# Moving the low parts of split operands to another start address modulo 512 bytes in SBUF

## What is computed

```python
def reference(x, ...):
    x = first_block(x, ...)    # layer 0: LRU + window attention, dense SwiGLU of width 2816
                               # layer 1: gated delta net, mixture of 8 experts of width 3584, top 2
    return second_block(x, ...)  # twice: SwiGLU of width 2816, conv/gating mixer, SwiGLU of width 2816

def swiglu(h, w_gate, w_up, w_down):
    return (jax.nn.silu(h @ w_gate) * (h @ w_up)) @ w_down
```

## Time and profile before

| | |
|---|---|
| median of the runs | 2406.1 us |
| span of the profiled execution, first to last instruction | 2403.7 us (2.4 us under the median of the runs) |
| PE busy | 2382.4 us, 99% of the span, 12542 matmuls |
| PEld busy | 2017.0 us, 84% |
| DVE busy | 1872.4 us, 78% |
| ACT busy | 1438.0 us, 60% |
| HBM | 597.91 MB read, 252 GB/s over the span |
| PE in the chain that ended last | 94% |

### The profile page before, as it was taken

The page is one execution under the profiler, slowest core; times in us unless marked ns, Lnnn a source line. Parts: engine busy times, 40 slices in busy tenths (PEclk is TensorE's granted clock), DMA queues, the critical chain, the costliest instruction groups (busy, mean ns, idle before and its releaser), DMA issues.

```text
span 2403.7 us, 34175 instructions
## 1 busy us (share of the span) xinstructions
PE 2382.4 (99%) x12542; PEld 2017.0 (84%) x12542; DVE 1872.4 (78%) x1961; ACT 1438.0 (60%) x1474; POOL 14.2 (1%) x34
## 2 busy tenths in 40 slices
PE   8999999999999999999999999999999999999998
PEld 7788899888888888888888888888788888897887
DVE  7767786678888888888888898677966676688666
ACT  6645455567777777777777776555254454544444
POOL 1000000000000000000000010000000000000000
PEclk9999999999999999999999999999999999999999
DMA  8375143459999999999999996853355566533653
GB/s 301 116 251 177 68 147 130 146 207 376 380 377 348 374 379 378 348 377 377 377 348 373 381 395 246 278 177 123 132 193 175 194 227 230 176 126 123 200 191 125
DMA packets 315952, 603.73 MB, mean 251 GB/s; under 512 B 9120, under 2 KB 135200, under 8 KB 315552
## 3 DMA queue, kind: packets, MB, share of 16 engines
q1 hardware_dynamic: 314160, 592.70, 69.1%
q10 hardware_dynamic: 1136, 7.87, 0.8%
q0 software_dynamic: 576, 2.10, 0.2%
HBM read 597.91 MB, written 8.91 MB: 252 GB/s over the span
## 4 chain that ended last, share of the span: by engine, by line
PE 94%; DVE 2%; ACT 1%; DMA 1%; DVEq 1%; issue 0%; SPq 0%; ACTq 0%
PE bank L205 20%; PE bank L206 20%; PE bank L207 19%; PE bank L1218 17%; PE bank L1222 9%; PE bank L3513 1%; PE bank L2955 1%; PE bank L3440 1%; PE bank L2230 1%; PE bank L2240 1%; DMA mslot<-in_e_w_in 1%; PE bank L2930 1%; PE bank L1714 1%; PE bank L1058 0%; PE bank L2149 0%; PE bank L2249 0%
## 5 line engine op out<-in xcount | busy, mean ns | idle before, releaser
L3205 DVE TENSOR_TENSOR weights_lo<-mslot,weights_hi 128x2048 fp32r<-128x2048 f32 x336 | 767.5, 2291 | 117.5 <-ACT weights_hi L3098 116.5
L3098 ACT ACTIVATE weights_hi<-mslot 128x2048 fp32r<-128x2048 f32 x336 | 644.0, 1919 | 217.4 <-PE bank L207 214.2
L1370 DVE TENSOR_TENSOR weights_lo<-scratch,weights_hi 128x2048 fp32r<-128x2048 f32 x165 | 377.2, 2289 | 166.3 <-ACT weights_hi L1363 166.2
L1218 PE MATMUL bank<-x_parts,weights_hi 128*128 128x512 f32 x1760 | 441.2, 392 | 1.8 <-DVE x_parts L921 1.8
L1218 PEld LDWEIGHTS bank<-x_parts,weights_hi 128*128 128x128 f32 x1760 | 319.4, 189 | 63.8 <-DVE x_parts L921 2.4
L205 PE MATMUL bank<-weights_hi,x_pair 128*128 128x512 f32 x896 | 356.9, 398 | 0.2 <-issue 0.2
L206 PE MATMUL bank<-weights_lo,x_pair 128*128 128x512 f32 x896 | 351.4, 392 | 0.0
L207 PE MATMUL bank<-weights_hi,x_pair 128*128 128x512 f32 x896 | 349.9, 391 | 0.0
L1363 ACT ACTIVATE weights_hi<-scratch 128x2048 fp32r<-128x2048 f32 x165 | 315.3, 1914 | 49.3 <-PE bank L207 49.0
L205 PE MATMUL bank<-weights_hi,hidden_hi 128*128 128x512 f32 x808 | 315.9, 391 | 0.0
L206 PE MATMUL bank<-weights_lo,hidden_hi 128*128 128x512 f32 x808 | 315.2, 390 | 0.0
(11 more groups left out here) (561 smaller groups left out, 2735.0 us busy)
## 6 DMA issues: line engine op xcount, KB each, us to landing
mslot<-in_o_moe_w_gate SPq DMA_DIRECT2D x112, 1024.0 KB, 6.8
mslot<-in_o_moe_w_up SPq DMA_DIRECT2D x112, 1024.0 KB, 6.8
mslot<-in_o_moe_w_down SPq DMA_DIRECT2D x112, 1024.0 KB, 6.9
scratch<-in_ffn_w_gate SPq DMA_DIRECT2D x44, 1024.0 KB, 5.2
scratch<-in_ffn_w_up SPq DMA_DIRECT2D x44, 1024.0 KB, 5.1
scratch<-in_ffn_w_down SPq DMA_DIRECT2D x44, 1024.0 KB, 5.0
mslot<-in_o_w_in SPq DMA_DIRECT2D x7, 2048.0 KB, 10.8
scratch<-in_e_ffn_w_gate SPq DMA_DIRECT2D x11, 1024.0 KB, 5.2
```

The costliest lines, as they stand in the source:

```text
L1218: pe.matmul(m.ps[bank + j][:, :], hi[:, k, cols(j)], both, start=(k == 0), stop=False)
L1370: dve.tensor_tensor(m.wlo[to][:, :], m.fslot[i], m.whi[to][:, :], ALU.subtract).then_inc(m.sig["f_lo"], 1)
L3098: act.activation(m.whi[(place + half) % PLACES][:, :], r.slot[slot + half], ACT.Copy).then_inc(s["r_hi"], 1)
L3205: dve.tensor_tensor(m.wlo[i][:, :], r.slot[slot + half], m.whi[i][:, :], ALU.subtract).then_inc(s["r_lo"], 1)
```

## The change

No instruction is added, removed or moved, and no semaphore wait changes: on every engine the same operations stand in the same order with the same shapes. Only addresses in SBUF change. These are the starts in bytes within each partition, modulo 512, as they follow from the widths in `place` (the rows and slices used in the products step by 512 bytes or multiples of it, so that each operand of a matmul has the number of its buffer):

| operand | before | after |
|---|---|---|
| weights_hi, x_parts, hidden_hi, fp32r scratch of the mixers | 64 | 64 |
| weights_lo | 64 | 128 |
| hidden_lo | 64 | 128 |
| x_pair, high half | 256 | 64 |
| x_pair, low half | 256 | 128 |
| mixer_lows (low parts of the mixer's last part) | 256 | 128 |
| mix_parts, mslot | 128 | 128 |
| fslot (raw FFN weights) | 256 | 64 |
| xn_lo | 64 | 64 |

A pad of 16 elements ("phase0") ahead of `weights_lo` and one of 112 behind it ("phase1") do this; `hidden_lo` goes into the room of the first mixer's gate weights `w_a` in `small`, 40 elements into it; `x_pair` gets 16 elements between its halves. The delta net's output product takes its buffers by an offset into `scratch` that keeps them at 64.

```diff
--- before.py
+++ after.py
@@ -48,6 +48,9 @@
 NE, FE = 8, 3584
 FC = 512
 NC = FE // FC
+
+PHASE = 16
+HL_AT = 40
 
 DA, DB, DC = 384, 256, 384
 AT = DA // P
@@ -138,6 +141,8 @@
     m.mslot = [sb(f"mslot{i}", KT * HALF) for i in range(3)]
     m.res = cut(sb("res", NT * D), 0, NT, D)
     consts = sb("consts", CONST_W)
+    with nc.sbuf_tensor("small_parts", [P, SMALL_W], F32R) as small_parts:
+        m.hl = cut(small_parts, SMALL_COLS["w_a"][0] + HL_AT, HALF)
     small = sb("small", SMALL_W)
     small2 = sb("small2", LAYERS2 * SMALL2_W)
     m.consts, m.small, m.small2 = consts, small, small2
@@ -173,24 +178,28 @@
         m.scr = lambda at, *dims: cut(scratch, at, *dims)
     with nc.sbuf_tensor("scratch_parts", [P, R], F32R) as scratch_parts:
         m.scr_parts = lambda at, *dims: cut(scratch_parts, at, *dims)
-    f0 = R - 3 * PIECE
+    f0 = 17408
     m.odd_rows, m.odd_xT = m.scr(21504, NT, D), m.scr(2048, KT, SEQ)
 
     m.splits = {u: i for i, u in enumerate((1, 4, 6, 7, 9))}
     rows = m.xn.rearrange("p t d -> p (t d)")
     m.diag, m.scales = rows[:, 0:SEQ], rows[:, SEQ:2 * SEQ]
-    m.c_raw = [m.scr(f0 + i * KT * DC, KT, DC) for i in range(2)]
+    m.c_raw = [m.scr(f0 + 16 + i * KT * DC, KT, DC) for i in range(2)]
     m.fslot = [m.scr(f0 + i * PIECE, PIECE) for i in range(3)]
 
     m.whi = [sb(f"weights_hi{i}", PIECE, F32R) for i in range(3)]
+    sb("phase0", PHASE)
     m.wlo = [sb(f"weights_lo{i}", PIECE, F32R) for i in range(3)]
+    sb("phase1", P - PHASE)
     m.x2 = cut(sb("x_parts", KT * 2 * SEQ, F32R), 0, KT, 2, SEQ)
     m.xh, m.xl = m.x2[:, :, 0, :], m.x2[:, :, 1, :]
-    m.hh, m.hl = sb("hidden_hi", HALF, F32R), sb("hidden_lo", HALF, F32R)
-    with nc.sbuf_tensor("mixer_lows", [P, f0 + 3 * PIECE - 6 * PIECE - KT * 2 * SEQ - 2 * HALF], F32R) as lows:
-        m.c_low = [cut(lows, f0 - 6 * PIECE - KT * 2 * SEQ - 2 * HALF + i * KT * DC, KT, DC) for i in range(2)]
-    sb("scratch_rest", f0 + PIECE - 6 * PIECE - KT * 2 * SEQ - 2 * HALF)
-    m.xg = cut(sb("x_pair", 2 * PIECE, F32R), 0, 2, KT, 2 * P)
+    m.hh = sb("hidden_hi", HALF, F32R)
+    free = f0 - 6 * PIECE - KT * 2 * SEQ - HALF - P
+    with nc.sbuf_tensor("mixer_lows", [P, free + 16 + 3 * PIECE], F32R) as lows:
+        m.c_low = [cut(lows, free + 16 + i * KT * DC, KT, DC) for i in range(2)]
+    sb("scratch_rest", free + PIECE)
+    xg = sb("x_pair", 2 * PIECE + PHASE, F32R)
+    m.xg = [cut(xg, i * (PIECE + PHASE), KT, 2 * P) for i in range(2)]
     return m
 
 
@@ -496,11 +505,10 @@
     ks = slice(half * KT // 2, (half + 1) * KT // 2)
     wide = lambda t: t.rearrange("p (k n) -> p k n", n=HALF)
     if b == 9:
-        hi = m.xg.rearrange("p i k t -> p (i k t)")[:, PIECE - 48:2 * PIECE - 48] if half == 0 else \
-            m.x2.rearrange("p k i t -> p (k i t)")[:, 0:PIECE]
+        hi = m.scr_parts((21504, 12288)[half], PIECE)
         low = m.b_low
     else:
-        hi = (m.whi[0], m.wlo[1])[half][:, :]
+        hi = (m.whi[0][:, :], m.scr_parts(8192, PIECE))[half]
         low = wide(m.mix[:, 2 * KT * HALF:3 * KT * HALF])
     return mblock(m, B_ODD + b)[:, ks, :], wide(hi), low[:, ks, :]
 
@@ -509,7 +517,7 @@
 
 
     turned = lambda x: x[:, :].rearrange("p (k t) -> p k t", t=SEQ)[:, :, t * P:(t + 1) * P]
-    return odd_mem(m).yT[:, :, t * P:(t + 1) * P], turned(m.wlo[2]), turned(m.wlo[0])
+    return odd_mem(m).yT[:, :, t * P:(t + 1) * P], turned(m.scr_parts(10240, PIECE)), turned(m.scr_parts(6144, PIECE))
 
 
 def odd_out_hi(act, m, b, half):
@@ -2790,7 +2798,7 @@
     flat = lambda t: t.rearrange("p k t -> p (k t)")
     x2 = m.x2.rearrange("p k i t -> p (k i t)")
     r.yh, r.yl = (x2[:, (2 + i) * KT * P:(3 + i) * KT * P] for i in range(2))
-    r.xg = [m.xg[:, i] for i in range(2)]
+    r.xg = m.xg
     xT = flat(m.xT)
     r.silu, r.h = xT[:, 0:FC], xT[:, FC:2 * FC]
     r.oh = m.oh.rearrange("p (t s) -> p t s", t=NT)
@@ -3410,7 +3418,7 @@
     c = Place()
     c.apad = m.scr(4096, AT, PAD_A + SEQ)
     c.sg = c.acc = m.scr(5120, AT, SEQ)
-    c.mixT = m.scr(10240, KT, SEQ)
+    c.mixT = m.scr(10240 + PHASE, KT, SEQ)
     c.g, c.v = m.scr(0, NT, 2 * DB), m.scr(1024, NT, DB)
     c.ccs, c.zacc = m.scr(1536, AT, SEQ), m.scr(13312, AT, SEQ)
     c.zpad = m.scr(14080, AT, PAD_C + SEQ)
```

## The result

The changed kernel takes **2417.6 us** (median of 5 runs, 2417.45 to 2419.08), against 2406.1 us before it (5 runs on the same chip, 2405.7 to 2407.0): a ratio of 1.0047, with a 95% interval from 1.0036 to 1.0057. It is 11.5 us slower, where 12 us less were forecast, and it lies outside the range (2386 to 2401 us).

A forecast was written before the change was run, and what follows sets the result against it. The prediction took PE's matmul pace, set by load-to-stream start offsets, as the bound. It summed 8.0 + 5.4 + 0.9 - 1.2 - 1.1 = 12.0 us, from 2406.1 to 2394 us, with a range for 8 in 10 of 2386 to 2401.

The forecast's parts named there:

- The rival by which they don't: Whole kernel: the address is not the cause of the slower pace, so nothing moves, 2406 us; chance 0.08.
- Step 3: Both downs: hidden_lo and weights_lo go to 128 together, load-to-stream offsets stay 0, 0, 0; zero gain.
- Step 2: Experts' gate and up: all three load-to-stream offsets go from 192 to 0; 896 triples gain 5.4 us.
- Step 1: FFN gate and up: load-to-stream offset goes from 0 to 64, a run of eight from 0.95 to 0.907; gain 8.0 us.
- Step 4: Mixer's last part: 64 triples go to offsets 64, 64, 64, from 0.354 to 0.340 us each; gain 0.9 us.
- Step 5: Last downs with hidden parts in x_parts: 80 triples get offsets 0, 448, 0, from 0.680 to 0.695; loss 1.2 us.
- Step 6: FFN: the 512-column matmul before each narrow run covers a load at offset 64; loss 1.1 us, bounded 0 to 3.3.
- The settling: FFN wide runs after narrow ones: 0.027 us extra expected to stay, not counted; 5.9 us more if it went.
- The third rival: Triples of 512 columns: the moving stream's jump between parts costs 0.015 us on all 896 + 808, giving 2422.8 us; chance 0.08.

The follow-up runs named there:

- wl_back: The changed kernel with weights_lo back at 64, while hidden_lo and x_pair's low half stay at 128; 2418.7 us, ratio to before 1.0052.
- all_at_64: The changed kernel with weights_lo, hidden_lo and both halves of x_pair at 64; 2401.8 us, ratio to before 0.9981.
- map1: A separate small program streaming only fp32r matmuls, with starting bytes as the one variable; 24 matmuls of 512 columns took 5.60 us at offset 64, 5.46 at 256.
- x_back: The changed kernel with hidden_lo and both halves of x_pair at 64, while weights_lo stays at 128; 2422.0 us (one run).
- narrow_alone: The all_at_64 kernel with only the FFN's gate and up low weight parts moved 64 bytes off x_parts; 2398.8 us, ratio to before 0.9969.
- ffn_phases: The all_at_64 kernel with FFN gate and up weights moved: high parts 192 bytes off x_parts, low parts 64; 2393.9 us, ratio to before 0.9949.
- low_256_off: The changed kernel with weights_lo, hidden_lo and x_pair's low half 256 bytes off the high parts instead of 64; 2401.4 us, ratio to before 0.9981.

## Why the prediction was wrong

The bound was read rightly: PE's pace is the time, no wait moved, and the start addresses do set the pace. The rival by which they don't is out: wl_back and all_at_64 differ in the starts of hidden_lo and of x_pair's low half alone, and by 17 us. The sentence of the Trainium skill (TensorE: Matmul & The Clock Gate, Step-by-step: what each phase is for) that a load doesn't steal read bandwidth doesn't carry as far as "addresses are free": the same matmul takes 0.2267 or 0.2333 us in map1, with nothing but the start of the stationary operand changed (L19 and L20).

- **Step 3, "Offsets stay 0, 0, 0. Zero.", is the step that failed.** It took the load's offset against the stream as the whole of the rule. down kept all its offsets and still went from 0.680 to 0.693, +8.2 us. What matters as well is that the triple's starts agree among themselves; a difference of 64 bytes broke that on both operands at once, and either alone costs as much (map1, wl_back, x_back).
- **Step 2** failed by the same rule. The half of it that moved x_pair to the weights' start was right: alone it gives 4.8 us in the sum of the triples (5.4 forecast). The half that spread the low parts cost 9.8 (627.1 against 617.3), so +5.0 came out.
- **Step 1** had the right sign and the wrong size: 0.942 for a run of eight instead of 0.907, 2.1 us over the 210 counted runs instead of 8.0 over 220. Its clean price came from a mixer stretch in which every matmul has the same offset. The FFN's narrow runs stand behind a wide run at offset 0, and behind such a run offset 64 gives 0.118 a matmul; behind one at 192 it gives 0.113 (narrow_alone and ffn_phases).
- **Step 4** gave nothing, 0.353 before and after. There too an offset of 64 in each of three places didn't bring 0.340. The same part has 16 triples with the high parts in `mix_parts`, which the prediction left out: their low parts moved too, and they went from 0.340 to 0.353, 0.2 us lost.
- **Step 5** came out as forecast: a median of 0.696 a triple for 0.695, and 1.0 us lost for 1.2. Its reason, the load at offset 448, isn't shown by that, since the stream jumps in these triples too.
- **Step 6** was too careful: the wide runs in front, the place of its entry, kept their sum (386.2 us against 386.4), and the last matmul of each, which now covers a load at offset 64, takes 0.227 us in the mean as before.
- **The settling** of 0.027 us in each wide run stayed, as said.

The third rival came nearest. Its sign was right, and its time, 2422.8 us, is 5 us off: the price a triple was 0.010 in the mean (8.2 us by 808) and not 0.015, the gains set against it shrank, and the 4.8 us that x_pair's new start gives were not in it. Its cause was too narrow, since the stationary side alone does the same (wl_back). The row that should have weighed more is the triple with the moving jump, with 0.695 the slowest of those that the prediction read: it changed two things at once, the jump and one load's offset, and the prediction put all of it on the one and gave the other a chance of 0.08, while the sum rested for 1704 triples on that choice. It was not the slowest triple of the kernel, as the prediction says: those of the second mixer's output product take 0.682 to 0.703, with a stream that doesn't jump. Had they been read, they would have pointed to the stationary side.

What stays open is what inside the chip the starts act on. The runs show pace alone. At the granted 2.4 GHz the three slower offsets cost 16, 12 and about 5 periods a matmul (6.7, 5.0 and 2.2 ns), for which no rule was found. Why the state that one run leaves reaches through the eight matmuls of the next was seen and not explained.

## What to carry to other kernels

Where split products of 512 columns in fp32r run back to back, let all operands of one product, high and low, moving and stationary, start at the same address modulo 256 bytes; move a buffer by multiples of 256 bytes if it has to move. For 256 columns this is not the best: offset 0 was the slowest there (0.120 us a matmul), and the fastest kernel, ffn_phases, has the FFN's gate and up parts at other starts. A pair of rows that differ in two things prices neither. When a sum rests on it a thousand times, the other reading deserves more than a small chance, and so does a "zero" for the largest group that the change touches.

Take a price from the place at which it will be paid, with the same work in front of it: 0.113 and 0.118 us were both the pace of one matmul with one offset.

## What the runs showed of the chip

- 512 columns of fp32r by start of the load against the stream: 0.2267 us at 0 and 256 bytes, 0.2333 at 64, 0.2317 at 128, 0.2288 at 192 (map1). The same figures came with the stationary operand 80 KB below the moving one in SBUF instead of 35 KB above it (L35 to L38: 5.48, 5.60, 5.58, 5.51 us for 24), so it is the start modulo 256 bytes and not the region.
- 256 columns: 0.120 us at offset 0, and 0.118 or 0.113 at 64 and 192, by what ran before (map1, L72 to L81).
- In a triple of 512 columns, a start that differs costs 0.007 to 0.020 us and mostly 0.013, for either operand; 256 bytes cost nothing (map1, low_256_off).
- Going from 256 to 512 columns with all loads at offset 0, the first five matmuls take 233, 236, 228, 233 and 231 ns before the pace settles at 227 (L82 of map1, and 71 places of the kernel before).
